# Gating the recurrence tile by tile: outputs with tokens on partitions, and an output projection that takes its slabs one after the other

## The reference, cut to what matters

```python
S_end, o = lax.scan(gdn_chunk_step, S0, (q, k, v, g, beta chunks))
o = o.reshape(B, L, GDN_HEADS, GDN_DV)                       # 8 heads of 128
o = rms_norm(o, norm_g) * jax.nn.silu(z)                     # per token and head
out = o.reshape(B, L, GDN_V) @ w_out                         # 1024 x 1024
# then: x = layer_norm(ALPHA * x + (1.0 + gate) * out, ...)  # gate = third part of silu(c) @ ada_w[0] + ada_b[0]
```

## Time and profile before

| what | value |
|---|---|
| median of three runs | 3372.42 us |
| profiled execution | 3364.95 us |
| its span | 3362.9 us |
| PE busy | 3139.0 us (93%) |
| DVE busy | 1894.7 us (56%) |
| ACT busy | 1065.2 us (32%) |
| POOL busy | 932.3 us (28%) |

### The profile page before, as it was taken

One profiled execution on the slowest core, in us unless ns is written; L12 is line 12 of the kernel. 1 busy time (PEld: TensorE's weight loads), 2 busy tenths in 40 slices (PEclk: granted clock), 3 DMA queues, 4 the chain that ended last, 5 costly groups with the idle time before them and its releaser, 6 DMA issues. The chain is left out here.

```text
span 3362.9 us, 51096 instructions
## 1 busy us (share of the span) xinstructions
PE 3139.0 (93%) x18954; PEld 2905.6 (86%) x18954; DVE 1894.7 (56%) x2879; ACT 1065.2 (32%) x1954; POOL 932.3 (28%) x646
## 2 busy tenths in 40 slices
PE   6999988999799999999999888989799999999996
PEld 2999988999388999999998777767789999999994
DVE  3899966776315555545556754434346455554555
ACT  1222224554214422222222633333235222222224
POOL 0322215664232322222223121000124222222222
PEclk8999988999699999999999999999899999999998
DMA  4545552210310111111111110000211111111111
GB/s 200 170 160 171 202 172 57 62 53 20 127 38 26 50 44 44 44 44 44 44 44 39 50 49 26 32 20 33 78 38 38 44 44 44 45 49 44 44 38 53
DMA packets 86935, 220.30 MB, mean 66 GB/s; under 512 B 9365, under 2 KB 42973, under 8 KB 85669
## 3 DMA queue, kind: packets, MB, share of 16 engines
q1 hardware_dynamic: 34164, 127.07, 11.3%
q10 hardware_dynamic: 52656, 91.67, 8.3%
HBM read 189.97 MB, written 28.75 MB: 65 GB/s over the span
## 5 line engine op out<-in xcount | busy, mean ns | idle before, releaser
L341 PE MATMUL PS<-HH,WH 128*128 128x354 f32 (+1 forms) x3528 | 1160.8, 329 | 80.3 <-issue 23.1
L345 PE MATMUL PS<-HH,WL 128*128 128x354 f32 (+1 forms) x3528 | 1151.9, 326 | 0.0
L344 PE MATMUL PS<-HL,WH 128*128 128x354 f32 (+1 forms) x3528 | 1151.2, 326 | 0.0
L337 POOL TENSOR_TENSOR WL<-RAW,WH 128x1024 fp32r<-128x1024 f32 x193 | 507.2, 2628 | 1111.1 <-ACT WH L332 1111.1
L341 PEld LDWEIGHTS PS<-HH,WH 128*128 128x128 f32 x3528 | 671.0, 190 | 97.6 <-issue 81.7
L344 PEld LDWEIGHTS PS<-HL,WH 128*128 128x128 f32 x3528 | 671.5, 190 | 2.2
L345 PEld LDWEIGHTS PS<-HH,WL 128*128 128x128 f32 x3528 | 669.7, 190 | 0.0
L1731 DVE SCALAR_TENSOR_TENSOR X<-PS,ADA,X 128x354 f32<-128x354 f32 (+1 forms) x704 | 329.7, 491 | 436.4 <-PE PS L345 435.6
L332 ACT ACTIVATE WH<-RAW 128x1024 fp32r<-128x1024 f32 x199 | 211.1, 1061 | 553.6 <-PE PS L341 553.3
L341 PE MATMUL PS<-FH,WH 128*128 128x354 f32 (+1 forms) x960 | 326.1, 340 | 9.9 <-DVE X L1731 9.8
L1706 DVE SCALAR_TENSOR_TENSOR CF<-UF,PSF,CF 128x1060 f32<-128x1060 f32 x176 | 331.7, 1940 | 0.0
(11 more groups left out here) (295 smaller groups left out, 3948.2 us busy)
## 6 DMA issues: line engine op xcount, KB each, us to landing
RAW<-ws SPq DMA_DIRECT2D x199, 512.0 KB, 3.6
ADR<-wada ACTq DMA_DIRECT2D x72, 512.0 KB, 4.8
scr<-V ACTq DMA_DIRECT2D x32, 530.0 KB, 3.5
AD<-wada SPq DMA_DIRECT2D x4, 2048.0 KB, 23.9
X<-xT SPq DMA_DIRECT2D x1, 4240.0 KB, 17.3
ZL<-scr ACTq DMA_DIRECT2D x8, 530.0 KB, 3.4
scr<-OH ACTq DMA_DIRECT2D x8, 530.0 KB, 2.7
KF<-scr ACTq DMA_DIRECT2D x8, 512.0 KB, 4.0
```

The source lines that it names most:

```text
L337: e.tensor_tensor(WL[u][:, :], RAW[:, u, :], WH[u][:, :].bitcast(fp32), ALU.subtract).then_inc(lo_done, 1)
L341: mm = e.matmul(out, WH[w][:, c:c + 128], mh, start=first, stop=False)
L344: e.matmul(out, WH[w][:, c:c + 128], ml, start=False, stop=False)
L345: return e.matmul(out, WL[w][:, c:c + 128], mh, start=False, stop=last)
```

## The change

1. `pe_oo` swaps its operands, so that the output of a tile has tokens on partitions. `act_out` copies it into one of two buffers OB instead of OUTT.
2. Norm and gate happen inside the loop, for each tile: ACT squares OB head by head with an accumulator output (`act_squares_out`, 8 instructions, at level 2), DVE adds epsilon (`vec_so`, 2 small ones, level 3), POOL takes the power -1/2 (`pool_ro`), DVE multiplies OB by it (`vec_scale`, level 4), PE transposes the 8 heads back to features (`pe_to_features`, three tiles later, level 0), and DVE multiplies by norm weight and silu(z) (`vec_gated`, 2 instructions).
3. silu(z) is read in one transfer of all eight blocks into OUTT, by SP, ahead of GB of the third tile, once the matmuls of the adaLN gate are done. `vec_gated` works in place.
4. The adaLN gate moves into the loop: its weights ADG are loaded by SP after the last dense group of the input projection, its matmuls stand behind levels 0 to 3 of tile 0 (`pe_ada_gate(e, n)`), its transposes behind level 5 (`pe_ada_columns`).
5. The first loads of keys, queries and values are issued by SP, earlier, instead of by ACT.
6. The split of the gated outputs is done chunk by chunk: upper part into HL (ACT), lower part into HH in place (DVE). The first slab of w_out starts with chunk 0 as soon as its tiles are ready; the last tile's transposes stand behind chunk 1. The weights of the first slab are loaded once `pe_sn` of tile 7 is done.
7. VB and AQ have two buffers instead of three, GAM lies elsewhere; the input `rows` goes.

```diff
@@ pe_oo
-                    out = PS[:, FA + g, (h % 4) * 128:(h % 4) * 128 + P]
-                    e.matmul(out, S[:, h, :], QE[i % 3][:, h, 0:P], start=True, stop=False)
-                    mm = e.matmul(out, VB[i % 3][0:P, h, :], AQ[i % 3][0:P, h, 0:P], start=False, stop=True)
+                    out = PS[0:P, FA + g, (h % 4) * 128:(h % 4) * 128 + 128]
+                    e.matmul(out, QE[i % 3][:, h, 0:P], S[:, h, :], start=True, stop=False)
+                    mm = e.matmul(out, AQ[i % 2][0:P, h, 0:P], VB[i % 2][0:P, h, :], start=False, stop=True)
@@ new on PE
+        def pe_to_features(e, i, b):
+            e.wait_ge(on_rdy, i + 1)
+            for g in G2:
+                for h in heads(g):
+                    mm = e.transpose(PS[:, b + g, (h % 4) * 128:(h % 4) * 128 + P], OB[i % 2][0:P, h, :], con(C_ID, P, P))
+                mm.then_inc(tr_ps, 1)
@@ pe_gdn, in the loop over levels n of tile i, and behind the loop
+                    if n == 0 and i >= 3:
+                        e.wait_ge(aq_rdy, 2 * (i + 1))
+                        pe_to_features(e, i - 3, FB_)
...
+                    if i == 0 and n < 4:
+                        pe_ada_gate(e, n)
+                    if i == 0 and n == 5:
+                        pe_ada_columns(e)
+            e.wait_ge(pp_rdy, lv(LAST, NL - 1, 1))
+            pe_to_features(e, LAST - 2, 0)
             pe_ks(e, LAST)
             pe_ur(e, LAST)
             pe_oo(e, LAST)
             pe_sn(e, LAST)
+            e.wait_ge(og_rdy, 2 * (LAST - 1))
+            pe_to_features(e, LAST - 1, 0)
@@ act_gdn
+        def act_squares_out(a, i):
+            for h in range(HEADS):
+                ins = a.activation(SQ[1][0:P, h, :], OB[i % 2][0:P, h, :], ACT.Square, accum_out=SSO[0:P, 8 * i + h:8 * i + h + 1])
...
+                    if n == 2 and b >= 1:
+                        act_squares_out(a, b - 1)
+                    if i == 0 and n == 4:
+                        act_ada_gate(a)
...
+            act_squares_out(a, LAST - 1)
+            act_out_upper(a, 0, 0)
+            act_out_upper(a, 0, 1)
+            split_hi(a, S_WO, S_WO % 2)
             act_w(a, LAST, 0)
             act_w(a, LAST, 1)
+            act_out_upper(a, 1, 0)
             act_out(a, LAST)
+            act_squares_out(a, LAST)
+            act_out_upper(a, 1, 1)
...
+            split_hi(a, S_WO + 1, (S_WO + 1) % 2)
+            act_out_upper(a, 2, 0)
+            act_out_upper(a, 2, 1)
@@ vec_gdn, behind the loop
             vec_r(v, LAST)
+            vec_so(v, LAST - 1)
+            vec_gated(v, LAST - 2, 0)
+            vec_out_lower(v, 0, 0)
+            vec_out_lower(v, 0, 1)
+            vec_scale(v, LAST - 1)
             vec_s(v, LAST)
+            vec_gated(v, LAST - 1, 0)
+            vec_so(v, LAST)
+            vec_out_lower(v, 1, 0)
+            vec_out_lower(v, 1, 1)
+            vec_scale(v, LAST)
+            vec_gated(v, LAST, FB_)
+            vec_out_lower(v, 2, 0)
+            vec_out_lower(v, 2, 1)
@@ pe_proj
+            if q == 0:
+                for ch in range(NCH):
+                    ready(ch, 0)
+                    dense_chunk(e, n0, n0 % 2, g0, g0 % 2, ch, ch == 0, mh, ml)
+                    if ch == 1:
+                        e.wait_ge(s_rdy, 2 * LAST + 2)
+                        pe_to_features(e, LAST, FB_)
+                ready(0, 1)
@@ pe_rest, act_rest, pool_rest, vec_rest: pe_gate, act_gate, pool_gate, vec_gate are gone
@@ SP
             load(S_WO - 1, 0)
+            need(sp, ada_sum, QKVB + ZB)
...
+            load_kq(sp, 0)
+            load_v(sp, 0)
+            load_kq(sp, 1)
+            need(sp, up_done, 3 * (QKVB + ZB) + 3)
+            for j in range(2):
+                sp.dma_start(ADG[j][:, :, :], wada0[:, 4 + j, :, :]).then_inc(ada0_ld[j], 16)
             sp.wait_ge(gx, 9)
             sp.dma_start(gsc, GTR[0:8 * (GT + 1), :]).then_inc(gt_st, 16)
...
                 sp.dma_start(GB[:, :, :], gsc[8 * i:8 * i + 8, :]...).then_inc(gb_ld, 16)
+                if i == 1:
...
+                    sp.wait_ge(ada0_row, 6)
+                    sp.dma_start(OUTT[:, :, :], scr[QKVB:QKVB + ZB, :, :].rearrange("b p t -> p b t")).then_inc(z_ld, 16)
-            sp.wait_ge(oo_rdy, GT + 1)
-            sp.wait_ge(s_rdy, 2 * GT + 2)
+            sp.wait_ge(sn_ps, 2 * LAST)
             load(S_WO, 1)
```

More of the change, by code:

```diff
@@ L685, in vec_ada, with pe_ada_gate, pe_ada_columns @@
             v.wait_ge(ada_done, 2)
[L687 to L694, removed]
-                    mm = e.matmul(PS[0:2, j, :], SC[:, k, :], ADG[j][:, k, :], start=(k == 0), stop=(k == KB - 1))
+        def pe_ada_gate(e, n):
+            j = n // 2
+            if n == 0:
+                e.wait_ge(aq_rdy, 2)
+            e.wait_ge(ada0_ld[j], 32)
+            for k in range(KB // 2 * (n % 2), KB // 2 * (n % 2 + 1)):
+                mm = e.matmul(PS[0:2, FB_ + j, :], SC[:, k, :], ADG[j][:, k, :], start=(k == 0), stop=(k == KB - 1))
+            if n % 2:
                 mm.then_inc(ada0_row, 1)
-            e.wait_ge(rb_ev, 24)
+        def pe_ada_columns(e):
+            e.wait_ge(uf_rdy, 2)
             for m in range(KB):
@@ L1099, in act_sqq @@
             a.wait_ge(t1q_ps, 2 * i + 2)
+            past(a, so_rdy, i - 3)
             if i:
@@ L1283, in vec_aq, with vec_so, vec_scale, vec_gated @@
                 v.wait_ge(kq_ps, 2 * i + g + 1)
-                v.tensor_tensor(grp(AQ[i % 3], g, P)[:, :, 0:P], bank(FB_ + g, P, P), grp(GAM, g, P)[:, :, 0:P], ALU.mult).then_inc(aq_rdy, 1)
+                v.tensor_tensor(grp(AQ[i % 2], g, P)[:, :, 0:P], bank(FB_ + g, P, P), grp(GAM, g, P)[:, :, 0:P], ALU.mult).then_inc(aq_rdy, 1)
+        def vec_so(v, i):
+            P = TP[i]
+            r = RSO[0:P, 8 * i:8 * i + 8]
+            v.wait_ge(so_rdy, i + 1)
+            v.scalar_tensor_tensor(r, SSA[0:P, 16 * i:16 * i + 8], 128.0 * 128.0 * RMS_EPS, SSO[0:P, 8 * i:8 * i + 8],
+                                   ALU.mult, ALU.add).then_inc(sv_rdy, 1)
+            v.wait_ge(sv_rdy, 2 * i + 1)
+            v.tensor_scalar(r, r, 1.0 / 128, 128.0 * RMS_EPS * RMS_EPS, ALU.mult, ALU.add).then_inc(sv_rdy, 1)
+        def vec_scale(v, i):
+            P = TP[i]
+            v.wait_ge(ro_rdy, i + 1)
+            v.tensor_tensor(OB[i % 2][0:P, :, :], OB[i % 2][0:P, :, :], RSO[0:P, 8 * i:8 * i + 8].unsqueeze(2).to_broadcast([P, 8, 128]),
+                            ALU.mult).then_inc(on_rdy, 1)
+        def vec_gated(v, i, b):
+            P, t0 = TP[i], tile_start(i)
+            v.wait_ge(z_ld, 16)
+            for g in G2:
+                o = OUTT[:, 4 * g:4 * g + 4, t0:t0 + P]
+                v.wait_ge(tr_ps, 2 * i + g + 1)
+                v.scalar_tensor_tensor(o, bank(b + g, 128, P), PAR[:, P_GNG:P_GNG + 1], o, ALU.mult, ALU.mult).then_inc(og_rdy, 1)
+        def vec_out_lower(v, ch, half):
+            c0, cw = CHS[ch]
+            b = slice(4 * half, 4 * half + 4)
+            v.wait_ge(oh_rdy, 2 * ch + half + 1)
+            v.tensor_tensor(HH[:, b, c0:c0 + cw], OUTT[:, b, c0:c0 + cw], HL[:, b, c0:c0 + cw].bitcast(fp32), ALU.subtract).then_inc(ol_rdy, 1)
         def vec_gdn(v):
@@ L1299, in vec_gdn @@
                         vec_s(v, b)
+                    if n == 0 and i >= 3:
+                        vec_gated(v, i - 3, FB_)
                     if n < TL[i]:
@@ L1445, in pool_gate @@
             split_lo(p, S_WO, S_WO % 2)
-            for h in range(HEADS):
-                p.wait_ge(oh_rdy, h + 1)
-                p.tensor_tensor(HL[:, h, :], OG[:, h % 2, :], HH[:, h, :].bitcast(fp32), ALU.subtract).then_inc(ol_rdy, 1)
+            pool_ro(p, LAST)
         def act_split_run(a, n0, n):
@@ L1459, in pe_proj @@
         def pe_proj(e, q, n0, g0, ready):
[L1460 to L1461 removed]
+            mh, ml = (HL, HH) if q == 0 else (HH, HL)
+            if q == 0:
[6 more added lines that the diff above has]
+                ready(0, 1)
+            for m in range(1 if q == 0 else 0, KB - 2):
+                dense(e, n0 + m, (n0 + m) % 2, g0 + m, (g0 + m) % 2, ready if m == 0 else None, KB, mh, ml)
             for ch, i in pe_tail(e, q, 2, 1):
                 m = KB - 2 + i
[L1464 removed]
+                dense_chunk(e, n0 + m, (n0 + m) % 2, g0 + m, (g0 + m) % 2, ch, (ch, i) in ((0, 0), (2, 1)), mh, ml)
         def vec_proj(v, q, s, g0):
@@ L2426, in _ @@
             load(S_WO - 1, 0)
+            need(sp, ada_sum, QKVB + ZB)
+            for u in range(2):
+                need(sp, v_st[u], 16 * QKVB // 2)
+            load_kq(sp, 0)
[4 more added lines that the diff above has]
+                sp.dma_start(ADG[j][:, :, :], wada0[:, 4 + j, :, :]).then_inc(ada0_ld[j], 16)
             sp.wait_ge(gx, 9)
```

224 lines of the change are left out of this document (99 added, 125 removed).

## The result

The changed kernel takes 3310.81 us (median of four runs, 3309.24 to 3313.14) against 3372.07 us for the kernel before (four runs, 3364.26 to 3372.95): ratio 0.9824, 95% interval 0.9807 to 0.9841. The profiled execution took 3311.9 us, with a span of 3310.4 us. From profiled execution to profiled execution that is 53.1 us less, from median to median 61.3. The executions of the kernel before are the wider ones: they fall into two groups, about 3364 to 3367 and 3372 to 3374 us over all comparisons, with medians from 3366.86 to 3372.43, and its profiled one (3364.95) lies in the lower group; the changed kernel's three medians lie within 3310.81 to 3312.49. So 53 to 61 us is one saving, counted from two ends of that spread, and I explain the 52.5 us between the two spans.

The account below looks back on a forecast made before the run. PE was taken to bound the loop, with 86 us passing in the gate stage behind it. PE's shifts, mainly the tail's -74.4, summed to -56.5 us; counted from the median 3372.42 that gave 3316 us, range 3300 to 3331.

Parts of the forecast that it names:

- Tail: From the recurrence's end to the second output slab: slab starts 74.4 us earlier, 2.5 lost to clock; bounds -80 to -66.
- Rounds: Rounds of tiles 3 to 8: eight added transposes cost PE 0.87 us each round, +5.3 in all; other engines' work hidden.
- Rival 5: First output slab still starts only when everything is gated; three chunks behind the last tile, about +10, 3326 us; 3%.
- the rival of the full slot: Part of Rival 2: ACT's slot in the rounds doesn't hold, squares at 0.56 a pair, +5 us; 22% for Rival 2.
- Loop start: PE's first transposes no longer wait 4.08 us for loads, issued by SP before 480: -4.0; bounds -5 to -3.
- Round of tile 0: adaLN gate matmuls 16.3 plus small transposes 0.8, less 4.3 hidden in idle time and 4.3 from clock: +8.5.
- Wait for tile 2's keys: Before tile 2's key transposes PE waits for keys and queries issued beside z: 15 us less 5.6, +9.4.
- Rival 1: Loads share the DMA engines so that tile 2 waits hardly at all: 3304 us; 22%.
- Rest of tile 1: Behind the wait: +2.3 for half clock, -4.3 from `pe_oo` streaming 128 columns in fewer stalls (bounds 0 to -6).
- Behind the second slab: Everything after the second output slab's start: nothing changes, 0.
- Rivals 2, 3 and 4: Rival 2 has its line; 3: gate matmuls at half clock throughout, 3327 us, 5%; 4: loop stays at half clock, 3576, 3%.
- Rival 2: Hand-made slots don't hold: squares +5, or a lower meeting POOL or longer tail stall, +8 together: 3324 us; 22%.

Follow-up runs that it names:

- the chunk experiment: The changed kernel with all three chunks of the first output slab waiting for everything, tile 8's transposes first: 3319.21 us, ratio 0.9851 to the kernel before.
- the repeat: The changed kernel again without any edit: 3311.11 us, ratio 0.9829 to the kernel before; its round of tile 0 took 30.84 us.
- two experiments: The changed kernel with z issued one round later, behind tile 2's keys: 3299.48 us; and with z loaded in nine short-row pieces: 3311.06 us (one run).

## Why the prediction was right, step by step

The time of 3316 us (3300 to 3331) met 3310.8, and the direction and size followed from two terms that held: the tail and the rounds. That the sum came within 4.0 us of the measured shift is partly luck: the other places missed by +2.1, +3.6, -2.3, +3.2, +2.4 and -3.8 us, which mostly cancel.

- **Tail.** -71.9 forecast with its clock, -73.1 measured. Both waits came, 1.73 and 5.78 us for 3 and 6, with the half clock behind them: twenty matmuls of the last chunk at 0.29 start to start for 0.16 are 2.6 us, 2.5 forecast. Within it sizes were off that cancelled in part: the two lowers beside POOL's split took 5.35 us, the next two, without it, 3.18 (3.4 forecast); `vec_scale` took 3.42 beside POOL's second split, 1.21 without. So DVE loses 2.2 us to POOL at two places, where I had named one with 3 us spare. Little of it reached PE: the last state update began right behind `vec_scale`, about 0.7 us after its first heads were there (an estimate from PE's last products), and tile 8's transposes stand behind chunk 1, which ended later than the scaling. The split of the tail between its parts rests on the chunk experiment; its largest part, the norm inside the loop, was not undone alone. Rival 5 did not come: chunk 0 started at 877.23, behind tile 7's transposes, while tile 8 was not yet scaled.
- **Rounds.** +5.1 for +5.3; doubled transposes cost 0.88 us a round. The slot on ACT held: eight squares took 2.3 us, not 3.4, because a square with its accumulator read takes 0.29 us start to start where I had taken 0.43, so the rival of the full slot had less for it than I said.
- **Loop start.** This is the step that failed (-0.4 for -4.0): "Issued by SP before 480 they have landed: -4.0. ACT's six issues there become one, so nothing new is late." The loads had landed. But the 4 MB of gate weights moved to the same moment, and a store of 72 KB, which ACT waits for, took 9.7 us instead of 1.6. I had priced those weights only by whether they come in time, not by who is queued beside them. With the weights behind the store 3.9 us come back.
- **Round of tile 0.** +6.2 for +8.5 (+4.8 in the repeat). The product took 16.0 us as forecast (16.3); 10 us of it were hidden or came back as clock, I had counted 8.6.
- **Wait for tile 2's keys.** +12.6 for +9.4. That the keys wait because z's long rows are beside them is shown by two experiments, only the size was off. I took 442 GB/s for the shared transfer; it ran at 396 to 399. Queries landed 17.4 us after their issue (15 forecast), and PE reached them after 4.9 us, not 5.6. Rival 1, no wait, fails by this, though its argument on shares is half true: by rows, not by bytes.
- **Rest of tile 1.** +0.4 for -2.0. Of the clock's 2.3 us 1.8 came, in the three groups behind the wait. Of the 4.3 that I took off 1.5 came: the products behind `pe_oo` took 2.05 us instead of 3.59, since the granted clock stays at 1.00 there (0.52 before). `pe_oo` itself, of the 32-token tile, took the same 5.3 us with its operands swapped, where that of a 128-token tile takes 3.6. So more columns on the moving side did not shorten it; why it takes longer was not looked for.
- **Behind the second slab.** -3.8, and I had nothing there. No edit touches these layers. The kernel before runs stretches at half clock near 1015 and 1077 us where the changed one does not. This part, from the start of the second slab to the end of the span, lasts 2409.9 to 2412.2 us in the three runs of the changed kernel, up to 2415.2 in its variants, and 2413.7 before. So the 3.8 us are within what varies by itself; what sets off such a stretch was not found.
- **The base.** I counted from the median, 7.5 us over the profiled execution. That offset belongs to the kernel before (its two groups of times) and not to the changed one, whose profile lies 1 us above its median. Counted from the profile the forecast is 3308 against 3311.9: 3.5 us too low where the other was 5 us too high.
- **Rivals 2, 3 and 4.** Of 3 and 4, half clock in the gate product or in the whole loop: the clock was 0.50 in the gate's first part and after the wait, and 1.00 in every round from 601 us on. Neither came. Rival 2 came in small: nothing waited for the squares, POOL's splits did cost DVE 2.2 us twice, and the tail's waits, 7.5 us, stayed under the 9 forecast.

## What to carry to other kernels

A transfer that is moved has to be priced twice: by when it lands, and by every small transfer that is in flight beside it, since here a short-rowed load or store next to a long-rowed one waited for most of it, while the long one (z) lost 0.2 us; put the long one behind the small one with a wait. Such a placement has its own price: it pays only where the long one is still in time, as z and the gate's weights were. When a serial stage goes into a loop whose bound is another engine, only what it adds on the bounding engine is paid (here 0.87 us a round, and in all 5.1 against 73 at the end). Gains of a few us from one place should be read at that place in the trace, because clock phases further on move with it.

## What the runs showed of the hardware that I had not expected

- Two queues that were both full moved equal numbers of rows, whatever the rows' length (675 and 676 packets in 8 us, 2368 and 2333 with short rows). A store of 72 KB took 9.7 us beside a load of 4 MB, 1.6 and 1.8 us without. Landing of 512 KB with 512-byte rows: 4.0 us without a large load, 15.8 beside 4.2 MB in rows of 4240 bytes, 6.6 beside the same bytes in 512-byte rows; the latter lowered the total from about 397 to about 300 GB/s.
- The engine that issues a load can be held by it. While the DMA engines were full ACT's queue took, in the changed kernel, 9.96 us to issue the values behind z, and ACT's next copy stood for 8.12; with z later the same issue took 0.65:

```profile
542.02 9.96 ACTq L1077 DMA_DIRECT2D VF<-scr  x1
...
552.08 1.08 ACT L1083 ACTIVATE PP<-PS 128x512 f32<-128x512 f32 x2 [8.12 <-issue]
```

- Removing 13.5 us of waiting gave 11.6 at the end, adding 4.3 cost 8: half-clock stretches of a few matmuls in the dense layers lie at other places in each variant, and lengthened what follows the second output slab by 0 to 5 us against the changed kernel's first run.
